# Every feed-forward matmul of a two-layer decoder step made as two of 64 rows, with the sums in two PSUM banks

## The reference, cut to what matters

```
def swiglu(x, w_gate, w_up, w_down):
    return (jax.nn.silu(x @ w_gate) * (x @ w_up)) @ w_down

h = x + 0.5 * rms_norm(swiglu(rms_norm(x, f1_pre), f1_wg, f1_wu, f1_wd), f1_post)
p_all = rms_norm(h, m_pre) @ w_in      # then four mixers: convolution, gated linear attention,
...                                    # short convolution, attention
h = h + rms_norm(y @ w_out, m_post)
h = h + 0.5 * rms_norm(swiglu(rms_norm(h, f2_pre), f2_wg, f2_wu, f2_wd), f2_post)
```

## Time and profile before

| | us |
|---|---|
| median of 3 runs | 1229.58 |
| lowest, highest | 1221.17, 1231.56 |
| span of the profiled execution (its time as the page has it; nothing is given around it) | 1226.4 |
| TensorE matmul busy in it | 1127.0 |
| VectorE busy | 771.9 |
| ScalarE busy | 563.0 |
| GpSimd busy | 382.8 |

### The profile page before, as it was taken

The page is one execution under the profiler, slowest core; times in us unless marked ns, Lnnn a source line. Parts: engine busy times, 40 slices in busy tenths (PEclk is TensorE's granted clock), DMA queues, the critical chain, the costliest instruction groups (busy, mean ns, idle before and its releaser), DMA issues.

```text
span 1226.4 us, 25500 instructions
## 1 busy us (share of the span) xinstructions
PE 1127.0 (92%) x8736; PEld 1082.5 (88%) x8736; DVE 771.9 (63%) x994; ACT 563.0 (46%) x900; POOL 382.8 (31%) x451
## 2 busy tenths in 40 slices
PE   6999999887997799999989999998699949999996
PEld 6999999767897699999989999977588948999995
DVE  5666544999762666654476665469987527666546
ACT  5544544541253654554454445445313536544544
POOL 2222201456622322220122222124664333222202
PEclk9999999997798799999999999999978979999998
DMA  6655566322329465545435556734223393655552
GB/s 248 209 185 187 173 210 190 123 97 74 104 87 72 137 207 178 187 159 200 171 114 197 173 187 186 230 106 155 87 78 122 86 114 121 202 176 182 178 177 83
DMA packets 80265, 188.63 MB, mean 154 GB/s; under 512 B 25627, under 2 KB 36387, under 8 KB 80035
## 3 DMA queue, kind: packets, MB, share of 16 engines
q1 hardware_dynamic: 80162, 187.31, 50.4%
HBM read 183.93 MB, written 3.35 MB: 153 GB/s over the span
## 4 chain that ended last, share of the span: by engine, by line
PE 75%; DVE 9%; issue 7%; DMA 4%; ACT 2%; SPq 2%; POOL 1%; DVEq 0%; ACTq 0%; POOLq 0%
PE ub L287 22%; PE ub L288 22%; PE ub L289 22%; DMA raw<-in_w_gu 3%; DVE resid L945 2%; PE mb L594 2%; DVE w_lo L274 2%; DVE z_t L942 2%; PE mb L627 1%; SPq L365 1%; ACT w_hi L268 1%; DVE proj L1184 1%; PE ub L307 1%; PE ub L309 1%; PE ub L308 1%
## 5 line engine op out<-in xcount | busy, mean ns | idle before, releaser
L274 DVE TENSOR_TENSOR w_lo<-raw,w_hi 128x1024 fp32r<-128x1024 f32 x339 | 453.4, 1343 | 403.9 <-ACT w_hi L268 403.7
L287 PE MATMUL ub<-hg_hi,w_hi 128*128 128x264 f32 x1648 | 482.7, 293 | 26.1 <-DVE proj L1184 22.9
L268 ACT ACTIVATE w_hi<-raw 128x1024 fp32r<-128x1024 f32 x339 | 346.2, 1027 | 343.9 <-PE ub L289 264.3
L288 PE MATMUL ub<-hg_lo,w_hi 128*128 128x264 f32 x1648 | 476.2, 289 | 0.0
L289 PE MATMUL ub<-hg_hi,w_lo 128*128 128x264 f32 x1648 | 475.5, 289 | 0.0
L287 PEld LDWEIGHTS ub<-hg_hi,w_hi 128*128 128x128 f32 x1648 | 320.3, 194 | 35.1 <-DVE w_lo L274 31.5
L288 PEld LDWEIGHTS ub<-hg_lo,w_hi 128*128 128x128 f32 x1648 | 320.5, 194 | 0.3
L289 PEld LDWEIGHTS ub<-hg_hi,w_lo 128*128 128x128 f32 x1648 | 318.5, 193 | 0.0
L287 PE MATMUL ub<-act_hi,w_hi 128*128 128x264 f32 x704 | 200.5, 285 | 0.0
L289 PE MATMUL ub<-act_hi,w_lo 128*128 128x264 f32 x704 | 199.6, 284 | 0.0
L288 PE MATMUL ub<-act_lo,w_hi 128*128 128x264 f32 x704 | 199.1, 283 | 0.0
(11 more groups left out here) (231 smaller groups left out, 1285.9 us busy)
## 6 DMA issues: line engine op xcount, KB each, us to landing
raw<-in_w_gu SPq DMA_DIRECT2D x179, 512.0 KB, 3.9
raw<-in_w_dn SPq DMA_DIRECT2D x64, 512.0 KB, 3.7
raw<-in_w_in SPq DMA_DIRECT2D x44, 512.0 KB, 3.4
raw<-in_w_dn SPq DMA_DIRECT2D x32, 384.0 KB, 3.4
raw<-in_w_out SPq DMA_DIRECT2D x16, 512.0 KB, 3.4
pages<-in_cache_k SPq DMA_DIRECT2D x32, 128.0 KB, 2.2
pages<-in_cache_v SPq DMA_DIRECT2D x32, 128.0 KB, 2.7
con<-in_con SPq DMA_DIRECT2D x1, 1444.0 KB
```

Source lines behind the costliest of these rows:

```text
L268: eng.activation(w_hi[:, slot, 0:w], raw[:, slot, 0:w], ACT.Copy).then_inc(*sig("hi_ready", reps))
L274: eng.tensor_tensor(w_lo[:, slot, 0:w], raw[:, slot, 0:w], w_hi[:, slot, 0:w].bitcast(F32), ALU.subtract)\
L287: eng.matmul(out, a_hi, x_hi[:, k0 + k, :], start=(first and k == 0), stop=False)
L288: eng.matmul(out, a_hi, x_lo[:, k0 + k, :], start=False, stop=False)
```

## The change

Each matmul of a feed-forward part becomes two: one over partitions 0 to 63 of the weights and of the activations, one over partitions 64 to 127, issued in turn. The first sums in `ub[s]`, the second in `mb[s]`. So the bank's value is the sum of two banks, and it has to be added up. For gate and up ScalarE copies the `mb` half to SBUF (`gate_s`, `up_s`), VectorE adds the `ub` half to it, waits for that, and multiplies by 1/rms from SBUF. For down ScalarE copies the `mb` half to `z_t`, VectorE adds it into the `ub` bank in place, and ScalarE's square and scaling read that. Since unit 3's second half goes to `mb[3]`, which holds NORM, TensorE waits for the first of the two steps of 1/rms before unit 3. The mixer's matmuls (in and out phases) stay as they are.

```
+        def multiply_halves(eng, outs, slot, x_hi, x_lo, tiles, k0, first, last, reps, ready=None):
+
+            for k in range(tiles):
+                if ready:
+                    ready(k0 + k)
+                for w, x, term in ((w_hi, x_hi, 0), (w_hi, x_lo, 1), (w_lo, x_hi, 2)):
+                    for i in range(2):
+                        r = slice(64 * i, 64 * (i + 1))
+                        mm = eng.matmul(outs[i], w[r, slot, k * P:(k + 1) * P], x[r, k0 + k, :], start=(first and k == 0 and term == 0),
+                                        stop=(last and k == tiles - 1 and term == 2))
+            mm.then_inc(*sig("unit_done", reps))
...
-                    multiply_unit(pe, ub[s][:, 0:NT], s, hg_hi, hg_lo, KD, 0, True, True, reps)
+                    multiply_halves(pe, (ub[s][:, 0:NT], mb[s][:, 0:NT]), s, hg_hi, hg_lo, KD, 0, True, True, reps)
...
-                multiply_first(pe, l, gu, hg_hi, hg_lo, ub, [P] * GROUP, "hg_ready", 8 * (q - 1))
+                halves_first(pe, l, gu, "hg_ready", 8 * (q - 1))
...
+                pe.wait_ge(*at(l, "rh_ready", 2 * q + 1))
                 gate_up(0, 3, 1)
...
-                    multiply_unit(pe, ub[s // 3 % 2][:, 0:NT], s % RING, act_hi, act_lo, DN_TILES[part], 8 * part,
+                    b = s // 3 % 2
+                    multiply_halves(pe, (ub[b][:, 0:NT], mb[b][:, 0:NT]), s % RING, act_hi, act_lo, DN_TILES[part], 8 * part,
...  (ScalarE, gate and up, at every second unit, before Silu)
+                        act.wait_ge(S["unit_done"], l * UNITS + PHASES[gu][0] + i * 4 + s + RING)
+                        act.wait_ge(*at(l, "silu_ready", f * 22 + j - 1))
+                        act.activation(gate_s[:, b, :], mb[s - 1][:, 0:NT], ACT.Copy).then_inc(*sig("gu_half", reps))
+                        act.wait_ge(S["unit_done"], l * UNITS + PHASES[gu][0] + i * 4 + s + 1 + RING)
+                        act.wait_ge(*at(l, "act_ready", f * 22 + j - 1))
+                        act.activation(up_s[:, b, :], mb[s][:, 0:NT], ACT.Copy).then_inc(*sig("gu_half", reps))
...  (ScalarE, down)
+                        act.activation(z_t[:, b, :], mb[b][:, 0:NT], ACT.Copy).then_inc(*sig("y_half", reps))
+                        act.wait_ge(*at(l, "y_both", f * 8 + n + 1))
                         output_tile(l, q, n, ub[b], b, reps)
...  (VectorE, gate; up is the same with ub[s] and up_s)
-                        dve.tensor_tensor(gate_s[:, b, :], ub[s - 1][:, 0:NT], rs_h[:, :], ALU.mult)\
+                        dve.wait_ge(*at(l, "gu_half", f * 44 + 2 * j + 1))
+                        dve.tensor_tensor(gate_s[:, b, :], ub[s - 1][:, 0:NT], gate_s[:, b, :], ALU.add).then_inc(*sig("gu_both", reps))
+                        dve.wait_ge(*at(l, "gu_both", f * 44 + 2 * j + 1))
+                        dve.tensor_tensor(gate_s[:, b, :], gate_s[:, b, :], rs_h[:, :], ALU.mult)\
                            .then_inc(*sig("gu_read", reps))
...  (VectorE, down, after rest_unit)
+                    if s % 3 == 2:
+                        n, b = i * 4 + s // 3, s // 3 % 2
+                        dve.wait_ge(*at(l, "y_half", f * 8 + n + 1))
+                        dve.tensor_tensor(ub[b][:, 0:NT], ub[b][:, 0:NT], z_t[:, b, :], ALU.add).then_inc(*sig("y_both", reps))
```

More of the change, by code:

```diff
@@ L290, in multiply_unit, with halves_first @@
             mm.then_inc(*sig("unit_done", reps))
+        def multiply_halves(eng, outs, slot, x_hi, x_lo, tiles, k0, first, last, reps, ready=None):
[8 more added lines that the diff above has]
+            mm.then_inc(*sig("unit_done", reps))
         def unit_bank(n):
             return ub[n if n < 4 else n % 2]
+        def halves_first(eng, l, phase, ready, count):
+            for k in range(KD):
+                for s in range(GROUP):
+                    if k == 0:
+                        eng.wait_ge(S["split_done"], l * UNITS + PHASES[phase][0] + s + 1 + RING)
+                    if s == 0:
+                        eng.wait_ge(*at(l, ready, count + k + 1))
+                    for w, x, term in ((w_hi, hg_hi, 0), (w_hi, hg_lo, 1), (w_lo, hg_hi, 2)):
+                        for i in range(2):
+                            r = slice(64 * i, 64 * (i + 1))
+                            mm = eng.matmul((ub, mb)[i][s][:, 0:NT], w[r, s, k * P:(k + 1) * P], x[r, k, :],
+                                            start=k == 0 and term == 0, stop=k == KD - 1 and term == 2)
+                    if k == KD - 1:
+                        mm.then_inc(*sig("unit_done"))
         def multiply_first(eng, l, phase, x_hi, x_lo, banks, widths, ready, count):
@@ L965, in gate_up, with down @@
                         dve.wait_ge(*at(l, "act_ready", f * 22 + j - 1))
-                        dve.tensor_tensor(up_s[:, b, :], ub[s][:, 0:NT], rs_h[:, :], ALU.mult)\
+                        dve.wait_ge(*at(l, "gu_half", f * 44 + 2 * j + 2))
+                        dve.tensor_tensor(up_s[:, b, :], ub[s][:, 0:NT], up_s[:, b, :], ALU.add).then_inc(*sig("gu_both", reps))
+                        dve.wait_ge(*at(l, "gu_both", f * 44 + 2 * j + 2))
+                        dve.tensor_tensor(up_s[:, b, :], up_s[:, b, :], rs_h[:, :], ALU.mult)\
                            .then_inc(*sig("gu_read", reps))
                 steps(dve, gu, l, gate_up)
-                steps(dve, dn, l, lambda i, s, reps, lead: rest_unit(dve, lead, reps), 12)
+                def down(i, s, reps, lead):
+                    rest_unit(dve, lead, reps)
+                    if s % 3 == 2:
+                        n, b = i * 4 + s // 3, s // 3 % 2
+                        dve.wait_ge(*at(l, "y_half", f * 8 + n + 1))
+                        dve.tensor_tensor(ub[b][:, 0:NT], ub[b][:, 0:NT], z_t[:, b, :], ALU.add).then_inc(*sig("y_both", reps))
+                steps(dve, dn, l, down, 12)
                 boundary(l, q)
@@ L1429 @@
 PERS = {
+    "gu_half": 88, "y_half": 16, "gu_both": 88, "y_both": 16,
     "past": 336, "keys_in": 256, "stored": 240, "lfn_in": 16, "values_in0": 128, "values_in1": 128, "unit_done":
```

## The result

The change makes the kernel **slower**: median 1258.79 us of 4 runs (1251.40 to 1263.58) against 1227.47 of 4 runs before, a ratio of 1.0254 with a 95% interval of 1.0216 to 1.0291. I had predicted 1195 and faster. The profiled execution has a span of 1249.6, 23.2 longer than before.

A forecast was written before the change was run, and what follows sets the result against it. TensorE was taken as the bound, at 0.121 us a matmul, falling to 0.113 a pair. Terms -48 + 4.4 + 4.0 + 4 + 1.2 = -34 on 1226.4 gave span 1192, plus 3.2 for the median: 1195 us, range 1178 to 1260.

The forecast's parts named there:

- The step that failed: Feed-forward matmuls on TensorE: of each 0.121 us step, 0.110 is the stream and 11 ns the weight load.
- the term of -48 us: Gain in the feed-forward phases: 1512 matmuls a part at 0.113 instead of 0.121 us, 12.1 a part, 48 for four.
- The rows of the mixer: Mixer's fp32 matmuls: a pair of halves costs what one full matmul costs, 2 to 4 ns over its stream.
- The load link of halves: TensorE, from weight load to matmul: 0.106 to 0.11 us for halves instead of 0.12, shorter than the stream.
- the pair stays at today's pace: No-gain rival on TensorE: no gain, costs stay; 1243 us at 0.121 a pair, 1285 at 0.128; chance 0.2.
- sums in single file: Rival at PSUM: two halves' results leave one a cycle, pair 0.220, some 1830 us; chance 0.13 with sequencer and clock.
- the sequencer: Rival on TensorE: its sequencer cannot keep 28 ns an instruction for long; within the joint chance of 0.13.
- Loop turns: Gate and up loop: the body of 1920 loads and matmuls may not stay resident; cost 4 us, bounds 0 and 12.
- The start of a part: Unit 3 waits for Ln, 0.7 us, and unit 4 for its bank, 0.4; 1.1 a part, 4.4 for four.
- The end: Before a part's last square: a copy, an add of 0.43 and two semaphores; 1.0 us, 4.0 for four parts.
- The middle: Added VectorE and ScalarE work within the phases: hidden, cost 0, VectorE 4.7 of 5.4 us per two units.
- the changes between halves and whole rows: TensorE around the norms: 0.1 to 0.3 us a change, 1.2 for eight changes not already hidden.

The follow-up runs named there:

- The streams: Kernel before, with float32r matmuls of one shape each added after its last phase on TensorE alone (first run): 121.4 ns full, 121.5 a pair at 264 columns.
- the control with the kernel before: Kernel before, with its gate and up loop as five turns of 8 units instead of two of 20: 1221.07 us against 1221.07, ratio 1.0003.
- the run without the second sums: Changed kernel with the `mb` sums left out of the result, so without ScalarE's copies and VectorE's adds: 1242.10 us, ratio 1.0222 to the kernel before.
- the short loop: Changed kernel with 40 gate and up units as five loop turns of 8 instead of two of 20: 1227.33 us against 1216.26 for the kernel before, 1.0086.
- the run with streams of types: Kernel before, with float32r, bf16 and fp32 streams, full and in pairs, added after its last phase: at 264 columns 121.4, 112.5 and 222.5 ns.

## Why the prediction was wrong, point by point

**The step that failed** is "So 11 ns in each 121 are the weight load's, not the stream's". It set the step of 0.121 against a stream at one column a cycle that no row of float32r had shown, and gave the remainder to the next thing in the timeline. The streams show 0.450 ns a column and 3 ns fixed, and a load floor of 111.7, which is hidden under it. The load of the earlier trace rows starts when the matmul before it starts, so the chain of two links looks closed; but a load that waits for its turn and a load that sets the turn look alike there. Two streams of different width, or one with half the weight columns, tell them apart. With this the term of -48 us becomes 0: 63.98 and 63.99 a down phase.

**The rows of the mixer** were read rightly and carried over wrongly. A pair of fp32 halves does cost what one fp32 matmul costs, and so does a float32r pair. I took from it "2 to 4 ns over its stream", which holds for fp32 and bf16 (2.7), and applied it to a type whose stream costs 8% more.

**The load link of halves**, 0.106 to 0.11, was not shorter than that of full rows: with 128 moving columns both take 111.7. It was never the limit either, so it was worth nothing.

**The rival "the pair stays at today's pace"** came true, in its lower case, 0.121, which it priced at 1243. Its mechanism was not quite the one I gave it, since neither the load link nor disturbance between halves sets the pace. I gave it 0.2. The streams show nothing for the second half, 0.1 ns in 121 and in 234. My estimate of 0.121 from the Trainium skill, "TensorE: Matmul & The Clock Gate", section on measured speedup against the span model, put 10% of a stream on a second tile. It agrees in number and not in cause.

**The rivals "sums in single file" and the sequencer** fell: halves start 0 to 0.03 apart and a pair takes 0.121, so PSUM takes two streams of sums together, and a sequencer too slow for four instructions in 0.121 us would show as pauses; there are none in the down phase, and the clock is 1.00 there.

**Loop turns** were the second error. I had doubled the body to 1920, named the risk, and taken 4 us with an upper bound of 12, from the 3.08 of another engine's branch. They cost 20 us (1.0254 to 1.0086). The 0.15 us of the old branch was a median over jumps and exits; the jumps took 0.22 to 0.24. The bound failed on its size and on what stands behind the branch. The gaps at the four jumps alone sum to 12.5 us. In the first part the second gap of issue adds 1.9 us from start to start, and in the first and third parts the clock at 1.2 GHz behind the gap does the rest: beyond the gaps at the jumps, they lose 4.2 and 4.7 us. Some 1.5 of the 4.7 stand at the third part's start, where the clock was at 1.2 GHz from 637.8 on, as in the control with the kernel before. That the clock falls behind such a gap is only seen: behind 2.7 us in the first part (before the second gap) and behind 4.2 in the third, and behind all four of 3.9 to 4.2 in the run without the second sums. Why it held behind the other 2.7 and 2.9 I can't say.

**The start of a part**: 1.1 predicted, 1.22 measured in three parts and nothing in the third, where a wait of 3.8 that was there before covers it; 3.6 in all for 4.4. Its two terms were sized wrongly against each other: the wait before unit 3 was put at 0.7, and unit 4, put at 0.4 more, is held up by 0.1 at most (119.04 for 118.97). **The end**: 1.0 predicted, 0.90 measured, 3.6 for 4.0. **The middle**: 0 predicted, and 0 measured (119.04 for 118.97); VectorE grew to 68% of the span and was never the bound. These terms sum to 7.2 us in the trace, and the short loop's 1.0086 is 10.5 (6.8 to 14.0): 1.5 more stand in the stretches of the short loop, nearly all in the third part, where the control has them too. The rest can be the changes between halves and whole rows, for which I had allowed 1.2, or noise; no run separates them.

**Size and range.** With 0 for the pair, 7 to 8 for start and end and 20 for the turns, the sum from 1229.6 comes to 1257, for 1258.79 measured. The measured time lies inside the range of 1178 to 1260 only because the range reached to the no-gain rival with costs, and there near its end because the loop turns cost five times their term; that is luck. The forecast itself had the sign wrong.

## What to carry to other kernels

Before a remainder between an expected and a measured pace is put on a neighbour (here the weight load), find the pace's price per column for the same type: two widths of one stream give slope and fixed part, and a split that leaves the moving columns as they are can't touch the slope. When a change doubles the instructions of a loop body, price the jump back as a gap with what follows it, waits and clock, not as one branch. If the type of the operands sets the pace, give the terms that bear it a cheaper type, and group by type so that few changes are left.

## What the runs showed of the hardware that was not expected

- A float32r stream costs 0.450 ns a column, bf16 0.416, at the same full clock; with bf16 moving data in steps of two 117.3 for 264 columns instead of 112.5, while weights in steps of two cost nothing.
- A pair of 64-row matmuls into two banks takes what one of 128 rows takes, to 0.1 ns, for 128 to 512 float32r columns, and for bf16 and fp32 as well (112.5 and 222.5 for 264).
- A change of type between matmuls cost some 8 ns in a quiet stream (16 for two); in the feed-forward phases two cost 13 to 15.
- The two halves keep no common order: in the first run of streams the first matmul of rows 64 to 127 starts before the last of the stream of rows 0 to 63 ahead of it in the program.

```profile
1274.02 0.39 PE L720 MATMUL mb<-act_hi,w_hi 64*128 64x264 f32 x1
1274.14 0.28 PE L717 MATMUL ub<-act_hi,w_hi 64*128 64x264 f32 x1
```

- TensorE's branch back over 1920 loads and matmuls took 3.4 to 4.9 us, over 960 or fewer 0.21 to 0.25, and the instruction queue moved 2.13 MB instead of 0.95. Unrolled, the same work moved 2.00 MB and cost nothing that shows.
- In the run with streams of types the clock fell to 1.2 GHz while TensorE was busy without a pause, on pairs with 64 moving columns, and stayed there through the streams of 64 columns behind them. The fp32 pairs before them had run at full clock. Windows (columns as in the earlier trace rows) of the two stretches:

```profile
1310.00:1320.00 10.00, 10.00 (x118) 9.03 (x114) 0.00 (x0) 0.00 (x0) 0.00 (x0) 1.00 0.00 0
1322.00:1332.00 10.00, 10.00 (x57) 9.94 (x57) 0.00 (x0) 0.00 (x0) 0.00 (x0) 0.50 0.00 0
```
